# Feed-forward, first product with the weights as the stationary side: two transformer blocks on one core

## What is computed

```
f = jnp.square(jax.nn.relu(jnp.einsum('btd,df->btf', x, w_ff1[l])))
h = jnp.einsum('btf,fd->btd', f, w_ff2[l])
x = layer_norm(DEEPNORM_ALPHA * x + h, ln2_g[l], ln2_b[l])
```

## Time and profile before

| | us |
|---|---|
| median of 3 runs | 3581.68 (3581.08 to 3586.04) |
| the profiled execution, its own time | 3581.32 |
| its span in the trace | 3579.5 |
| PE busy | 3451.6 (96%) |
| DVE busy | 2182.7 (61%) |
| ACT busy | 1619.1 (45%) |
| POOL busy | 347.3 (10%) |

### The profile page before, as it was taken

The page is one execution under the profiler, slowest core; times in us unless marked ns, Lnnn a source line. Parts: engine busy times, 40 slices in busy tenths (PEclk is TensorE's granted clock), DMA queues, the critical chain, the costliest instruction groups (busy, mean ns, idle before and its releaser), DMA issues.

```text
span 3579.5 us, 43123 instructions
## 1 busy us (share of the span) xinstructions
PE 3451.6 (96%) x16363; PEld 2882.2 (81%) x16363; DVE 2182.7 (61%) x2439; ACT 1619.1 (45%) x1957; POOL 347.3 (10%) x222
## 2 busy tenths in 40 slices
PE   8999989999999999989999999999999878999999
PEld 7788778888888787877788888888888777888877
DVE  5986665555555688866655555566456643666654
ACT  4444444444444446443444443444446532455553
POOL 0034010000000001420200000000000141000100
PEclk9999999999999999999999999999999989999999
DMA  7645556666666665455666666656656400565634
GB/s 231 177 146 160 182 177 188 193 187 190 188 193 187 189 190 151 141 162 192 225 192 188 191 187 192 188 182 208 184 171 181 142 6 12 189 197 172 181 121 161
DMA packets 312154, 617.03 MB, mean 172 GB/s; under 512 B 19353, under 2 KB 19353, under 8 KB 310315
## 3 DMA queue, kind: packets, MB, share of 16 engines
q1 hardware_dynamic: 306960, 591.73, 54.2%
q0 software_dynamic: 5024, 22.88, 1.9%
HBM read 612.44 MB, written 2.10 MB: 172 GB/s over the span
## 4 chain that ended last, share of the span: by engine, by line
PE 85%; DVE 10%; ACT 3%; POOL 1%; DMA 1%; issue 1%; SPq 0%; DVEq 0%; ACTq 0%; POOLq 0%
PE ps_unit L263 25%; PE ps_unit L265 25%; PE ps_unit L264 25%; DVE sb_w_lo L247 3%; DVE sb_conv_y L1146 2%; PE ps_mix L2568 2%; PE ps_mix L1220 1%; PE ps_mix L795 1%; ACT sb_w_hi L240 1%; PE ps_mix L646 1%; DMA sb_raw<-in_w_in_dram 1%; PE ps_mix L2566 0%; PE ps_mix L291 0%; DVE sb_x L422 0%; PE ps_mix L2923 0%
## 5 line engine op out<-in xcount | busy, mean ns | idle before, releaser
L247 DVE TENSOR_TENSOR sb_w_lo<-sb_raw,sb_w_hi 128x1024 fp32r<-128x1024 f32 x1120 | 1419.0, 1280 | 1035.3 <-ACT sb_w_hi L240 1030.2
L240 ACT ACTIVATE sb_w_hi<-sb_raw 128x1024 fp32r<-128x1024 f32 x1120 | 1177.3, 1059 | 1433.4 <-DMA sb_raw<-in_w_ff_dram 719.4
L263 PE MATMUL ps_unit<-sb_w_hi,sb_a_hi 128*128 128x512 f32 x3456 | 1367.1, 396 | 27.9 <-DVE sb_w_lo L247 18.1
L265 PE MATMUL ps_unit<-sb_w_hi,sb_a_lo 128*128 128x512 f32 x3456 | 1352.0, 391 | 0.0
L264 PE MATMUL ps_unit<-sb_w_lo,sb_a_hi 128*128 128x512 f32 x3456 | 1351.0, 391 | 0.0
L263 PEld LDWEIGHTS ps_unit<-sb_w_hi,sb_a_hi 128*128 128x128 f32 x3456 | 653.4, 189 | 165.0 <-issue 16.2
L265 PEld LDWEIGHTS ps_unit<-sb_w_hi,sb_a_lo 128*128 128x128 f32 x3456 | 652.2, 189 | 138.4
L264 PEld LDWEIGHTS ps_unit<-sb_w_lo,sb_a_hi 128*128 128x128 f32 x3456 | 653.1, 189 | 131.5
L263 PE MATMUL ps_unit<-sb_w_hi,sb_f_hi 128*128 128x512 f32 x1024 | 400.0, 391 | 0.0
L265 PE MATMUL ps_unit<-sb_w_hi,sb_f_lo 128*128 128x512 f32 x1024 | 398.6, 389 | 0.0
L264 PE MATMUL ps_unit<-sb_w_lo,sb_f_hi 128*128 128x512 f32 x1024 | 398.4, 389 | 0.0
(11 more groups left out here) (460 smaller groups left out, 2065.5 us busy)
## 6 DMA issues: line engine op xcount, KB each, us to landing
sb_raw<-in_w_ff_dram SPq DMA_DIRECT2D x512, 512.0 KB, 3.7
sb_raw<-in_w_in_dram SPq DMA_DIRECT2D x224, 512.0 KB, 3.7
sb_raw<-in_e_w_in_dram SPq DMA_DIRECT2D x112, 512.0 KB, 3.5
sb_raw<-in_o_w_in_dram SPq DMA_DIRECT2D x112, 512.0 KB, 3.7
sb_raw<-in_w_out_dram SPq DMA_DIRECT2D x64, 512.0 KB, 3.7
sb_raw<-in_e_w_out_dram SPq DMA_DIRECT2D x32, 512.0 KB, 3.6
sb_raw<-in_o_w_out_dram SPq DMA_DIRECT2D x32, 512.0 KB, 3.6
sb_raw<-in_e_w_mem_kv_dram SPq DMA_DIRECT2D x16, 512.0 KB, 3.6
```

Of the source, the lines that this page charges most:

```text
L240: k.nc.scalar.activation(k.w_hi[:, j], k.raw[:, j], ACT.Copy).then_inc(k.hi_ready, 1)
L247: k.nc.vector.tensor_tensor(k.w_lo[:, j], k.raw[:, j], k.w_hi[:, j].bitcast(F32), ALU.subtract).then_inc(k.lo_ready, 1)
L263: k.nc.tensor.matmul(acc, hi[:, kt, tokens], w_hi, start=kt == 0, stop=False)
L265: last = k.nc.tensor.matmul(acc, lo[:, kt, tokens], w_hi, start=False, stop=kt == KT - 1)
```

## The change

The first product of the feed-forward is made with the sides exchanged. `pe_columns_block` takes 128 weight columns as the stationary side and lets all 256 tokens move: per block two row tiles, four pieces of 128 columns and three passes, so 24 matmuls of 256 columns in place of 12 of 512. The result has the columns of `f` on the partitions, as the second product needs it. A unit now has four results of 256 columns, each in a bank of its own; units alternate over the two sets of four banks (`column_banks`). Squares are no longer turned; ACT and DVE make `f_hi` and `f_lo` from `relu2`. Unit 0 of the first group of each layer keeps the old form and its turn. Unit 4 of the later groups takes two banks of `k.ps` (`output_bank`), and the turns of the memory move from unit 5 to unit 6. In the loops of ACT and DVE over groups the first group is now written out ahead.

```diff
--- before.py
+++ after.py
@@ -247,9 +247,10 @@
     k.nc.vector.tensor_tensor(k.w_lo[:, j], k.raw[:, j], k.w_hi[:, j].bitcast(F32), ALU.subtract).then_inc(k.lo_ready, 1)


-def pe_block(pe, k, b0, c, hi, lo, tiles=range(TT)):
+def pe_block(pe, k, b0, c, hi, lo, tiles=range(TT), bank=None):

     s, j = c // BLOCKS % 2, c % BLOCKS
+    bank = k.ps_unit[:, s] if bank is None else bank
     if 0 in tiles:
         if j == 0:
             pe.wait_ge(k.evacuated, b0 + (c + BLOCKS))
@@ -258,7 +259,7 @@
         kt = KB * j + n
         for t in tiles:
             tokens = slice(t * P, (t + 1) * P)
-            acc = k.ps_unit[:, s, t, :]
+            acc = bank[:, t, :]
             w_hi, w_lo = k.w_hi[:, j, n, :], k.w_lo[:, j, n, :]
             k.nc.tensor.matmul(acc, hi[:, kt, tokens], w_hi, start=kt == 0, stop=False)
             k.nc.tensor.matmul(acc, hi[:, kt, tokens], w_lo, start=False, stop=False)
@@ -624,11 +625,12 @@
     return k.nc.vector.scalar_tensor_tensor(x, x, scale, out, ALU.mult, ALU.add)


-def residual(dve, k, b0, u, chunk, scale=None):
+def residual(dve, k, b0, u, chunk, scale=None, bank=None):

     wait_unit(dve, k, b0, u)
     cols = bass.ds(chunk * NC, NC)
-    add_residual(k, k.x[:, :, cols], k.ps_unit[:, u % 2], scale).then_inc(k.evacuated, BLOCKS)
+    bank = k.ps_unit[:, u % 2] if bank is None else bank
+    add_residual(k, k.x[:, :, cols], bank, scale).then_inc(k.evacuated, BLOCKS)
     dve.wait_ge(k.evacuated, b0 + (u + 3) * BLOCKS)
     for t in range(TT):
         last = k.nc.vector.bn_stats(k.stats[:, t, bass.ds(chunk, 1), :].rearrange("p c s -> p (c s)"), k.x[:, t, cols])
@@ -779,21 +781,55 @@
                 sp.dma_start(k.raw[:, j], src).then_inc(k.raw_ready[j], 16)


+def column_banks(k, g0, u):
+
+
+    mixed = u % 2 == 1 if g0 == 0 else u % 2 == 0
+    banks = k.ps[:] if mixed else k.ps_unit[:].rearrange("p s t n -> p (s t) n")
+    return banks[:, :, 0:SEQ]
+
+
+def output_bank(k, g0, u):
+
+    return k.ps[:, 0:TT, :] if g0 and u == 4 else k.ps_unit[:, u % 2]
+
+
+def pe_columns_block(pe, k, b0, c, banks):
+
+
+    j = c % BLOCKS
+    if j == 0:
+        pe.wait_ge(k.evacuated, b0 + (c + BLOCKS))
+    pe.wait_ge(k.lo_ready, b0 + (c + 1))
+    for n in range(KB):
+        kt = KB * j + n
+        for x in range(NC // P):
+            cols = slice(x * P, (x + 1) * P)
+            w_hi, w_lo = k.w_hi[:, j, n, cols], k.w_lo[:, j, n, cols]
+            k.nc.tensor.matmul(banks[:, x, :], w_hi, k.a_hi[:, kt, :], start=kt == 0, stop=False)
+            k.nc.tensor.matmul(banks[:, x, :], w_lo, k.a_hi[:, kt, :], start=False, stop=False)
+            last = k.nc.tensor.matmul(banks[:, x, :], w_hi, k.a_lo[:, kt, :], start=False, stop=kt == KT - 1)
+    last.then_inc(k.block_done, 1)
+
+
+def by_columns(buffer, u):
+
+    return buffer[:, u % 2].rearrange("p t (c s) -> p (t c) s", c=NC // SEQ)
+
+
 def pe_feed_forward(pe, k, layer, tile, between=None, after=None):
     first = k.block0["pe"]
     k.block0["pe"] += FF_GROUPS * FF_UNITS * BLOCKS
     done = layer * FF_GROUPS * 4

-    def turn(n, u):
-
-
-        pe.wait_ge(k.relu2_ready, n + (u + 3))
-        pe.wait_ge(k.f_lo_ready, n + (u + 1))
+    def turn_first(n):
+
+
+        pe.wait_ge(k.relu2_ready, n + 3)
+        turned = turned_first_unit(k)
         for kt in range(4):
-            bank = k.ps[:, 2 * (u % 2) + kt // 2, :].rearrange("p (a s) -> p a s", a=2)
             for t in range(TT):
-                last = k.nc.tensor.transpose(bank[:, kt % 2, t * P:(t + 1) * P],
-                                             k.relu2[:, u % 2, t, kt * P:(kt + 1) * P], k.ident)
+                last = k.nc.tensor.transpose(turned[:, kt, t * P:(t + 1) * P], k.relu2[:, 0, t, kt * P:(kt + 1) * P], k.ident)
         last.then_inc(k.f_turned, 1)

     def group(q, g0, between=None):
@@ -811,28 +847,33 @@
             for j in range(BLOCKS):
                 if u == 4 and j == 0:
                     pe.wait_ge(k.f_lo_ready, n + 5)
-                if j == 4 and 1 <= u <= 4:
-                    turn(n, u - 1)
+                if j == 4 and u == 1 and g0 == 0:
+                    turn_first(n)
+                if j == 0 and u == 2 and g0 == 0:
+                    pe.wait_ge(k.f_lo_ready, n + 3)
                 if u == 4 and j == 6:
                     pe.wait_ge(k.f_lo_ready, n + 6)
                 if between:
                     between(u, j)
-                pe_block(pe, k, b0, u * BLOCKS + j, hi, lo)
+                if u < 4:
+                    pe_columns_block(pe, k, b0, u * BLOCKS + j, column_banks(k, g0, u))
+                else:
+                    pe_block(pe, k, b0, u * BLOCKS + j, hi, lo, bank=output_bank(k, g0, u))

     group(0, 0)
     for q in range(1, FF_GROUPS):
         group(0, q, between if q == FF_GROUPS - 1 else None)


-def turned_unit(k, u):
-    return k.ps[:, 2 * (u % 2):2 * (u % 2) + 2, :].rearrange("p b (a s) -> p (b a) s", a=2)
+def turned_first_unit(k):
+    return k.ps_unit[:, 1].rearrange("p b (a s) -> p (b a) s", a=2)


 def act_feed_forward(act, k, layer, between=None, root=None):
     first = k.block0["act"]
     k.block0["act"] += FF_GROUPS * FF_UNITS * BLOCKS
     done = layer * FF_GROUPS * 4
-    def group(q, between=None, root=None):
+    def group(q, g0, between=None, root=None):
         b0 = q * (FF_UNITS * BLOCKS) + first
         n = q * 4 + done
         for u in range(FF_UNITS):
@@ -841,9 +882,13 @@
                 if between:
                     between(u, j - AHEAD)
             if 1 <= u <= 4:
-                act.wait_ge(k.f_turned, n + (u + 2))
-                k.nc.scalar.activation(k.f_hi[:, 4 * (u - 1):4 * u, :], turned_unit(k, u - 1),
-                                       ACT.Copy).then_inc(k.f_hi_ready, 1)
+                if g0 == 0 and u == 1:
+                    act.wait_ge(k.f_turned, layer + 1)
+                    columns = turned_first_unit(k)
+                else:
+                    act.wait_ge(k.relu2_ready, n + (u + 2))
+                    columns = by_columns(k.relu2, u - 1)
+                k.nc.scalar.activation(k.f_hi[:, 4 * (u - 1):4 * u, :], columns, ACT.Copy).then_inc(k.f_hi_ready, 1)
             if root and u == FF_UNITS - 1:
                 act_split(act, k, b0, u * BLOCKS + AHEAD + 4)
                 act_seam(act, k, b0, FF_UNITS * BLOCKS, root)
@@ -855,11 +900,16 @@
             if u < 4:
                 wait_unit(act, k, b0, u)
                 act.wait_ge(k.relu2_ready, n + (u + 1))
-                k.nc.scalar.activation(k.relu[:, u % 2], k.ps_unit[:, u % 2], ACT.Relu).then_inc(k.evacuated, BLOCKS)
-
-    with act.Fori(0, FF_GROUPS - 1) as q:
-        group(q)
-    group(FF_GROUPS - 1, between, root)
+                if g0 == 0 and u == 0:
+                    to, unit = k.relu[:, 0], k.ps_unit[:, 0]
+                else:
+                    to, unit = by_columns(k.relu, u), column_banks(k, g0, u)
+                k.nc.scalar.activation(to, unit, ACT.Relu).then_inc(k.evacuated, BLOCKS)
+
+    group(0, 0)
+    with act.Fori(1, FF_GROUPS - 1) as q:
+        group(q, 1)
+    group(FF_GROUPS - 1, FF_GROUPS - 1, between, root)


 def pool_feed_forward(pool, k, layer):
@@ -871,7 +921,7 @@
         n = q * 4 + done
         for u in range(4):
             pool.wait_ge(k.evacuated, b0 + (u + 3) * BLOCKS)
-            pool.wait_ge(k.f_turned, n + (u + 1))
+            pool.wait_ge(k.f_lo_ready, n + (u + 1))
             k.nc.gpsimd.tensor_tensor(k.relu2[:, u % 2], k.relu[:, u % 2], k.relu[:, u % 2],
                                       ALU.mult).then_inc(k.relu2_ready, 1)
@@ -884,7 +934,7 @@
     if norm:
         k.stats_units += FF_GROUPS * OUT_UNITS

-    def group(q, between=None, norm=None):
+    def group(q, g0, between=None, norm=None):
         b0 = q * (FF_UNITS * BLOCKS) + first
         n = q * 4 + done
         for u in range(FF_UNITS):
@@ -895,7 +945,8 @@
             if 1 <= u <= 4:
                 dve.wait_ge(k.f_hi_ready, n + u)
                 part = slice(4 * (u - 1), 4 * u)
-                k.nc.vector.tensor_tensor(k.f_lo[:, part, :], turned_unit(k, u - 1), k.f_hi[:, part, :].bitcast(F32),
+                columns = turned_first_unit(k) if g0 == 0 and u == 1 else by_columns(k.relu2, u - 1)
+                k.nc.vector.tensor_tensor(k.f_lo[:, part, :], columns, k.f_hi[:, part, :].bitcast(F32),
                                           ALU.subtract).then_inc(k.f_lo_ready, 1)
             if norm and u == FF_UNITS - 1:
                 dve_split(dve, k, b0, u * BLOCKS + AHEAD + 4)
@@ -905,14 +956,15 @@
                 if u >= 4 and j == AHEAD + 7:
                     if u == 4:
                         dve.wait_ge(*scaled)
-                    residual(dve, k, b0, u, u - 4)
+                    residual(dve, k, b0, u, u - 4, bank=output_bank(k, g0, u))
                 dve_split(dve, k, b0, u * BLOCKS + j)
                 if between:
                     between(u, j - AHEAD)

-    with dve.Fori(0, FF_GROUPS - 1) as q:
-        group(q)
```

(11 more changed lines are left out.)

## The result

The changed kernel takes 3591.82 us (median of 7 runs, 3589.22 to 3596.48), the kernel before 3581.69 (median of 7). The ratio is 1.0024, with a 95% interval of 1.0013 to 1.0036: slower by 10 us, where 22 us less were forecast.

A forecast was written before the change was run, and what follows sets the result against it. The prediction took PE alone to bound the feed-forward. Turns -27.3, matmuls +5.0 and small waits +0.6 gave -21.7 us, so 3581.3 became 3559.6 us, with a range from 3552 to 3583.

The forecast's parts named there:

- What bounds the kernel: In the feed-forward, 600 to 1100 us, PE alone was said to set the time, busy for 500 of 500 us.
- The turns: Transposes between the feed-forward's products: 30 of 32 turns go, at 0.91 us each, all on PE's path, -27.3 us.
- The matmuls: First product: 5760 matmuls of 256 columns at 114.2 ns, the middle of 113.3 and 115.1, against 113.3 free: +5.0 us.
- the gate rows: Trace of the second stack's gate columns, 256 tokens moving, 24 columns loaded: 115.1 ns per step, taken as nearest in form.
- The small waits: Late starts at the 16 changes between the two matmul forms, some 0.04 us each, +0.6 us.
- those at 0: Waits for banks, relu, square, `f_hi`, `f_lo` and the moved memory turns in the feed-forward: all claimed hidden, 0 us.
- Rival 2: First product: load or fixed price decides, a new matmul takes 120 ns, +11.7 us in all, 3593.0 us; chance 8%.
- Rival 1: First product: uneven starts give the gain back, about 118 ns per new matmul, +0.2 us in all, 3581.5 us; chance 10%.
- Rival 3: First product: PE bound by being handed instructions, load and matmul about 125 ns, +40.7 us in all, 3622.0 us; chance 3%.
- The rule of the Trainium skill: Warm gap of N/2.4 + 2.5 ns per matmul: doubling the count costs 7.2 us, sum -20.1 us before small terms.

The follow-up runs named there:

- The streams: Two kernels of nothing but matmuls, form after form, 96 or 144 each, not the reference's computation; 256 moving by 128 stationary fp32r columns took 120.0 ns per step.
- the first stream: A kernel of its own with only streams of 96 matmuls per form, varying moving and stationary widths; 226.7 ns at 512 moving columns, 120.0 at 256.

## Why the prediction was wrong

**What bounds the kernel** was right: PE alone in this stretch, before and after, with the cover of all other engines whole.

**The turns, -27.3 us.** Right. The kernel without them measures -28.4, and their stretch is 2.74 us shorter for three.

**The matmuls, +5.0 us.** This is the step that failed: 114.2 ns were taken for one new matmul and it is 120.0, so the term is +38.4 us. The prediction had this value as an upper end ("about 120 ns if the 13.3 ns that a matmul of 512 columns takes beyond its 512 cycles were a fixed price of each") and put it aside because "the gate rows speak against" it. The streams show why they could not: with 24 to 112 stationary columns the price at 256 moving columns is smaller than with 128. The gate rows were nearest in what moves and far in what stands still. The second argument, that loads of 128 columns can follow each other every 111.5 ns, was true (111.6 and 111.7 in the streams) and beside the point: PE is not held by the load alone. The choice of the middle between two low ends rested on these two rows, each of which showed one half of the form; nothing had shown the two together, and the range should have reached to the fixed price. What the 120.0 ns consist of stays open: the price depends on the width of the stationary side, and no run separates it from the load.

**The small waits, +0.6 us, and those at 0.** The waits were right: the kernel without turns leaves exactly 87.04 us for 384 matmuls, and PE waits for nothing in the changed one between 600 and 1100 us. The 0.6 us were too much. In the trace of the changed kernel the first steps after a change to 512 columns are 27 ns late in all, and those after a change to 256 are 7 ns early, which is about 0.2 us for 8 groups.

**The rivals.** Rival 2 came true in its price (120 ns, 3593.0 us against 3591.8 measured). Neither of its reasons is shown as it stands. The load doesn't start late: in the changed kernel the next load starts 2 to 3 ns after a matmul's start, and so it does under the plain matmuls of L2568. The 13.3 ns are the same from 512 down to 256 moving columns at four widths, but not at 448, and they change with the stationary side, so a fixed price per matmul describes this form and not others. The rival's threshold was also reckoned wrong: by its own terms the kernel turns slower by 0.2% (7.2 us) from 119.2 ns on, not from 119.8; nothing in the sum or the range hangs on it. Rival 1 wanted uneven starts; the steps are even to the nanosecond. Rival 3 (PE bound by being handed instructions, 125 ns) falls: the streams take a load and a matmul every 111.6 ns, 192 in a row.

The rule of the Trainium skill that was weighed (TensorE: Matmul & The Clock Gate, Back-to-back issue gap) had the direction right, a fixed price per matmul that doubling the count pays twice. That section of the Trainium skill gives it for isolated matmuls and not for pairs of load and matmul, and its 2.5 ns are not what fp32r with a load before each matmul pays here: 13.3. The plain fp32 rows of the first stream come near it at one width only. 215.8 ns per recorded matmul of 256 columns is 2 x 106.7 + 2.5, but at 128 columns the step is 111.7, where 2 x 53.3 + 2.5 would be 109.2.

## What to carry to other kernels

Before halving the moving columns of a matmul that already keeps PE busy, write its step as N/2.4 plus a rest, and multiply the rest by the number of matmuls that will be added: here 13.3 ns x 2880 = 38.4 us, more than the 28.4 us of turns that it saved. A row is a measure for a new form only if both of its sides, the one that moves and the one that is loaded, have the new form's width; where none does, the extrapolation of the steady row itself belongs into the range. And where one operand meets two others, putting these side by side in one matmul of 512 columns gives a part of the rest back: here 11 us, and 19 with the widths grouped, against 25.6 if each matmul had kept its own step.

## What the runs showed of the hardware

- An fp32r matmul with 128 stationary columns takes its moving columns at 2.4 GHz plus 13.3 ns at 512, 384, 320 and 256; at 416, 448 and 480 columns 15.0, 20.0 and 16.7 ns (448 had 16.0 in the first stream).
- At 256 moving columns the addition falls with the stationary side: 13.3 ns at 128 columns, 11.1 at 112, 10.0 at 96, 6.7 at 80, 64, 48 and 32, but 10.8 at 24. At 512 it does not fall but rises, to 16.7 at 96 and 64 and 18.3 at 32 (17.5 in the first stream). What mechanism makes both is open.
- With 128 stationary columns the step is 111.7 ns at 192 and at 128 moving columns alike, so it is no longer the moving side that sets it. That it is the load is likely but not shown, as no narrower load was run at these widths. The transposes of a turn, which load 128 columns too, start 109 ns apart.
- Alternating 512 and 256 columns costs 353.3 ns a pair where each alone would give 346.7. In groups of eight the long steps are the first five after the change to 512.
- A plain fp32 matmul of the streams appears in the trace as two records, each with its own load: 96 in the program are 192 in the group above.
